# Byte offsets of split weights and activations in SBUF, and moved waits, in a one-core transformer kernel

## The reference

```
x = x + rms(retention(rms(x)))          # 4 heads; then x += (p0 @ W) * sigmoid(x @ Wg)
x = x + rms(latent_attention(rms(x)))   # 16 heads; then x += (p1 @ W) * sigmoid(x @ Wg)
mod = silu(c) @ w_ada + b_ada           # six rows of 1024 for shift, scale and gate
h = layer_norm(x) * (1 + sc1) + sh1
a, u, gates = h @ w_in                  # a: value and gate; u: 512 channels to be pooled
ya = silu(ln(conv31(a_val * sigmoid(a_gate)))) @ w_pw    # causal, depthwise, 31 taps, 512 channels
yb = multiscale_pool(u) @ w_pool * pool_scale
x = ln(ALPHA * x + g1 * ((sig(ga) * ya + sig(gb) * yb) @ w_out))
x = ln(ALPHA * x + g2 * ((gelu(gt) * v) @ w_down))       # v, gt from a conv with 3 taps of h @ w_up
```

## Time and profile before

| | |
|---|---|
| time, median of 3 runs | 846.46 us (845.76 to 847.8) |
| the profiled execution's own time | 850.78 us |
| its span, first to last instruction | 848.9 us |
| PE busy | 824.6 us (97%) |
| DVE, ACT, POOL busy | 664.1, 452.8, 46.8 us |
| data moved | 170.56 MB, mean 201 GB/s |

### The profile page before, as it was taken

How to read it: one execution, slowest core, us unless ns; L and a number is a source line. 1 busy time by engine, 2 the same in 40 slices (tenths; PEclk the granted TensorE clock), 3 DMA queues, 4 the chain that set the end, 5 groups by cost and what they waited for, 6 DMA issues and landing times.

```text
span 848.9 us, 14927 instructions
## 1 busy us (share of the span) xinstructions
PE 824.6 (97%) x5362; PEld 744.6 (88%) x5362; DVE 664.1 (78%) x1039; ACT 452.8 (53%) x678; POOL 46.8 (6%) x58
## 2 busy tenths in 40 slices
PE   9699999999999999999999999999999999999996
PEld 9598989888787999999987889988988999999884
DVE  5669896976874796877867777999798888888456
ACT  6353546464654656566565545202852877776440
POOL 0006300000010000000000000080000000000000
PEclk9899999999999999999999999999999999999998
DMA  6766684759754665564739662444663565566641
GB/s 236 258 219 223 199 286 168 271 182 351 262 172 152 217 224 183 192 231 143 271 112 359 203 238 86 162 156 148 212 208 126 185 211 189 182 203 217 196 151 50
DMA packets 49001, 170.56 MB, mean 201 GB/s; under 512 B 6080, under 2 KB 6720, under 8 KB 48960
## 3 DMA queue, kind: packets, MB, share of 16 engines
q1 hardware_dynamic: 40896, 143.23, 49.8%
q10 hardware_dynamic: 8064, 26.78, 9.0%
HBM read 168.93 MB, written 1.06 MB: 200 GB/s over the span
## 4 chain that ended last, share of the span: by engine, by line
PE 88%; DVE 4%; ACT 4%; DMA 2%; issue 1%; ACTq 0%; SPq 0%; DVEq 0%
PE bank L485 13%; PE bank L487 13%; PE bank L486 13%; PE bank L553 9%; PE bank L555 9%; PE bank L554 9%; PE bank L521 6%; PE bank L499 2%; PE bank L690 2%; PE bank L691 2%; PE bank L692 2%; DMA ada_raw<-ada_in 1%; PE bank L596 1%; PE bank L831 1%; DMA crow<-c_row 1%
## 5 line engine op out<-in xcount | busy, mean ns | idle before, releaser
L967 ACT ACTIVATE whi<-raw 128x1024 fp32r<-128x1024 f32 (+1 forms) x232 | 239.8, 1040 | 215.1 <-PE bank L487 92.4
L1492 DVE TENSOR_TENSOR wlo<-raw,whi 128x1024 fp32r<-128x1024 f32 (+1 forms) x232 | 278.3, 1212 | 74.3 <-ACT whi L967 72.8
L485 PE MATMUL bank<-H,whi 128*128 128x256 f32 x784 | 222.4, 284 | 0.1
L487 PE MATMUL bank<-H,wlo 128*128 128x256 f32 x784 | 219.4, 280 | 0.0
L486 PE MATMUL bank<-H,whi 128*128 128x256 f32 x784 | 218.6, 279 | 0.0
L485 PEld LDWEIGHTS bank<-H,whi 128*128 128x128 f32 x784 | 147.4, 188 | 1.0 <-issue 0.9
L486 PEld LDWEIGHTS bank<-H,whi 128*128 128x128 f32 x784 | 147.5, 188 | 0.1
L487 PEld LDWEIGHTS bank<-H,wlo 128*128 128x128 f32 x784 | 147.3, 188 | 0.0
L553 PE MATMUL bank<-whi,Y 128*128 128x512 f32 x216 | 86.0, 398 | 1.4 <-DVE wlo L1492 1.4
L555 PE MATMUL bank<-whi,Y 128*128 128x512 f32 x216 | 85.4, 395 | 0.0
L554 PE MATMUL bank<-wlo,Y 128*128 128x512 f32 x216 | 85.4, 395 | 0.0
(11 more groups left out here) (264 smaller groups left out, 1345.5 us busy)
## 6 DMA issues: line engine op xcount, KB each, us to landing
ada_raw<-ada_in ACTq DMA_DIRECT2D x48, 512.0 KB, 5.0
raw<-w_head SPq DMA_DIRECT2D x47, 512.0 KB, 4.4
raw<-w_up SPq DMA_DIRECT2D x42, 512.0 KB, 3.7
raw<-w_down SPq DMA_DIRECT2D x22, 512.0 KB, 4.3
raw<-w_uq SPq DMA_DIRECT2D x24, 384.0 KB, 3.1
raw<-w_ret_out SPq DMA_DIRECT2D x16, 512.0 KB, 5.5
raw<-w_mla_gate SPq DMA_DIRECT2D x16, 512.0 KB, 4.4
raw<-w_mla_out SPq DMA_DIRECT2D x16, 512.0 KB, 4.5
```

The lines of the kernel that those rows point to most:

```text
L485: mm(o, whi[:, s, c], a[:, 0, :], start=start, stop=False)
L487: last = mm(o, wlo[:, s, c], a[:, 0, :], start=False, stop=stop)
L967: activation(parts_of(b, n)[0], block_in(b, n), ACT.Copy).then_inc(hi_done, 1)
L1492: tt(lo, block_in(b, n), f32(hi), ALU.subtract).then_inc(lo_done, 1)
```

## The change

- `whi` and `wlo` get slots of 1088 elements instead of 1024 (4352 bytes). Blocks used as strips are written 16 elements (64 bytes) into their slot; `row_block` tells the row blocks, which are written at its first byte.
- `macc` grows from 32 to 256 bytes, so that the activations start at the same remainder by 256 as the slots.
- DVE's wait for `crow` moves from ahead of the first head into `ada`.
- In `out_rows` one `ada` goes behind `post_rows` and the next split, and the first two splits of `B_MO` move into the last head group, on ACT and on DVE; ACT takes two gate evacuations ahead of `turned(2)` there.
- At `B_MIN` the transposes of the second token tile start before the last half of the first pass's last block.
- PE's wait for `dve_free` before the groups moves into the group, ahead of the scores.
- Four blocks of `B_WG` (8 to 11) turn from plain products into strips: SP loads them, ACT and DVE split them, the last 14 taps interleaved with three of these splits. `conv_mean` comes behind the third of the eight strips, `conv_squares` behind the fifth.
- The running total of the taps is kept in PSUM (`CT`), and the last tap writes `CO`.

```diff
-        whi = sb("whi", [P, RING, 1024], F32R)
-        wlo = sb("wlo", [P, RING, 1024], F32R)
+        whi = sb("whi", [P, RING, 1024 + SLOT_PAD], F32R)      # SLOT_PAD, STRIP_AT = 64, 16
+        wlo = sb("wlo", [P, RING, 1024 + SLOT_PAD], F32R)
-        macc = sb("macc", [P, 8])
+        macc = sb("macc", [P, 64])
+        CT = PB[2][:].rearrange("p (c t) -> p c t", c=4)
+def row_block(b):
+    if b < B_RO:
+        return b % 12 in range(4, 8)
+    if B_GRP <= b < B_MO:
+        return (b - B_GRP) % 12 == 1
+    return b < B_MIN + 8 or B_MO <= b < B_WA or B_WO <= b < B_UP or b >= B_DN + 5
...
-            return whi[:, b % RING, 0:n], wlo[:, b % RING, 0:n]
+            o = 0 if row_block(b) else STRIP_AT
+            return whi[:, b % RING, o:o + n], wlo[:, b % RING, o:o + n]
...
-            load_plain_loop(B_WG, "gates", 4, 4)
+            load_plain_loop(B_WG, "gates", 3, 4)
+            load_some(B_WG, "gates", 12, 16)
...
-                    c = slice(t * P, t * P + P)
+                    c = slice(STRIP_AT + t * P, STRIP_AT + t * P + P)
...
-            token_pass(B_MIN, 0, 0, H, 0, 4, tile_waits(U_PRE1, 0))
-            turn_tile(U_PRE1, 1, WT, PB[1])
+            (blocks 0 to 2 of the pass, then:)
+            row_products(B_MIN + 3, half(2, 0, 0), 0, H, 6, False, True, (0,))
+            turn_tile(U_PRE1, 1, WT, PB[1], (0,))
+            row_products(B_MIN + 3, half(2, 0, 0), 0, H, 6, False, True, (1,)).then_inc(tok_done, 1)
+            turn_tile(U_PRE1, 1, WT, PB[1], (1,))
...
-            with pe.Fori(0, 3) as i:
+            with pe.Fori(0, 2) as i:
                 (four plain_tokens of B_WG)
-            conv_mean()
-            for j in range(12, 16):
+            for j in range(8, 16):
                 strip(B_WG + j, halves(b)[j % 2], H)
-                if j == 13:
+                if j == 10:
+                    conv_mean()
+                if j == 12:
                     conv_squares()
...
# ACT and DVE, out_rows:
-                    if base != B_RO or j > 1:
+                    if j > 1:
                         split(base + j)
# DVE:
+                dve.wait_ge(c_loaded, 16)        # in ada
...
-                    if j == 12:
-                        ada(ada0 + 6, 0, 6, 0, 0)
                 dve.wait_ge(row_a, loaded)
                 post_rows(n_root, 0, row)
                 split(base + 13)
+                ada(ada0 + 6, 0, 6, 0, 0)
...
-            dve.wait_ge(c_loaded, 16)            # ahead of the first head
...
+                        total = CO if per == 0 and k == CONV_K - 1 else CT
+                        stt(total[:, c, :], x, w_tap, CT[:, c, :], ALU.mult, ALU.add).then_inc(conv_tap[c], 1)
...
-            with dve.Fori(0, 7) as i:
+            with dve.Fori(0, 6) as i:
                 (14 taps)
+            for k in range(4):
+                if k < 3:
+                    split(B_WG + 5 + k)
+                (the last 14 taps, three or two a round behind each split)
...
             tt(CS[:, 0, :], CS[:, 0, :], CS[:, 1, :], ALU.add).then_inc(conv_sum, 1)
+            split(B_WG + 8)
```

More of the change, by code:

```diff
@@ L546, in loaded, with row_products @@
                 pe.wait_ge(lo_done, base + RING + 1)
-            def row_products(base, o, t, a, k0, start, stop):
+            def row_products(base, o, t, a, k0, start, stop, ks=(0, 1)):
                 hi, lo = parts_of(base)
-                for k in range(2):
+                for k in ks:
                     c = slice(512 * k, 512 * k + 512)
@@ L589, in hold, with turn_tile @@
                     mm(b[:, 0:P], ones[:], ones[:], start=True, stop=True)
[L591 to L593 removed]
+            def turn_tile(u, t, src, b, qs=(0, 1)):
+                for q in qs:
                     pe.wait_ge(wt_ready, 2 * (u + t) + q + 1)
@@ L736, in _ @@
                 row_products(B_PG0 + 4 + j, half(2, 1, 1), 1, H, 2 * j, j == 0, j == 3).then_inc(pe_done, 1)
-            token_pass(B_MIN, 0, 0, H, 0, 4, tile_waits(U_PRE1, 0))
-            turn_tile(U_PRE1, 1, WT, PB[1])
+            before = tile_waits(U_PRE1, 0)
+            for j in range(4):
+                loaded(B_MIN + j)
+                if j < len(before) and before[j]:
+                    pe.wait_ge(*before[j])
+                if j < 3:
+                    row_products(B_MIN + j, half(2, 0, 0), 0, H, 2 * j, j == 0, False)
+            row_products(B_MIN + 3, half(2, 0, 0), 0, H, 6, False, True, (0,))
+            turn_tile(U_PRE1, 1, WT, PB[1], (0,))
+            row_products(B_MIN + 3, half(2, 0, 0), 0, H, 6, False, True, (1,)).then_inc(tok_done, 1)
+            turn_tile(U_PRE1, 1, WT, PB[1], (1,))
             token_pass(B_MIN, 1, 0, H, 0, 4, tile_waits(U_PRE1, 1))
@@ L1323, in group @@
                     exps(3)
+                    split(B_MO)
+                    for j in range(2):
+                        gate_evac_one(base + 8 + j, j, 4 * o + 2 + j)
                     turned(2)
                     turned(3)
-                    for j in range(2):
-                        gate_evac_one(base + 8 + j, j, 4 * o + 2 + j)
+                    split(B_MO + 1)
                 act.wait_ge(mo_gated, at(5, 4))
@@ L1365, in _ @@
             evac(B_WP + 3, 1, U[:, 2:4, 16:16 + T], ACT.Copy)
-            with act.Fori(0, 2) as i:
-                evac(B_WG + 1, 0, dyn(G, 4 * i, 2), ACT.Sigmoid, 4, i)
-                evac(B_WG + 3, 1, dyn(G, 4 * i + 2, 2), ACT.Sigmoid, 4, i)
+            for n in range(3):
+                evac(B_WG + 2 * n + 1, n, pair(G, n), ACT.Sigmoid)
             act.wait_ge(pooled, 4)
             activation(Sh, PO, ACT.Copy).then_inc(pooled_hi, 1)
+            split(B_WG + 5)
+            split(B_WG + 6)
+            evac(B_WG + 7, 1, pair(G, 3), ACT.Sigmoid)
+            split(B_WG + 7)
+            split(B_WG + 8)
             evac(B_WG + 9, 0, pair(G, 4), ACT.Sigmoid)
```

22 lines of the change are left out of this document (14 added, 8 removed).

## The result

The changed kernel takes 824.75 us (median of 4, 823.85 to 828.66) against 846.61 us (median of 4, 845.76 to 847.8) in the same comparison: a ratio of 0.9749, 95% interval 0.9721 to 0.9778. It is 21.9 us faster. I had forecast 813.6 in a range from 796 to 832: the sign and the range hold, and the time is that of rival 3 (823) and not that of the forecast. The profiled execution has a span of 826.9 us, the longest of the five on record (the other four have 822.1 to 823.3). The profile of before, 850.78 us, is likewise of an execution above all its timed ones.

What follows compares the result with a forecast made beforehand. PE, busy 97% of the span, was taken as the bound. Addresses 17.8 - 0.5, `crow` wait 9.3, smaller pauses 2.7 and conv stage 3.6 sum to 32.9 us: from 846.46 to 813.6 us, range 796 to 832.

Steps and rivals of the forecast that it cites:

- rival 3: Only row blocks gain from the new addresses, strips stay at 116.7 ns a matmul; 823 us, chance 0.15.
- Rows of the address: Row blocks with moving operand in slots: 1176 matmuls of 512 columns gain 6.7 ns each, 7.8 us (0 to 20.3).
- Rival 1: The addresses do nothing, the kept blocks are fast for another reason; 831 us, chance 0.17.
- Strips of the address: Strips: 3000 matmuls of 256 columns go from 116.7 to 113.3 ns, 10.0 us less (0 to 26).
- split between strips and rows: Sign of a wrong forecast in the profile after: matmul pace unchanged, or differing between strips and row blocks.
- Rival 2: An address mismatch explains all PE lacks to the plain pace; 785 us, midway 799; chance 0.20 in whole or part.
- The wait for `crow`: PE's pause at 28.65 us and the half clock behind it: 7.4 + 2.4 - 0.5 = 9.3 us gained (6.9 to 9.8).
- Smaller pauses: PE's short waits before the projection, at `B_MIN` and at `B_MO`: together 2.7 us gained (1.5 to 3.2).
- Conv stage: Four plain blocks become strips, taps in PSUM avoid POOL's cost, the wait before `B_PW` goes: net 3.6 us gained.
- The overlap: Address gain lost where another engine sets the end: some 0.5 us in the conv stage, room elsewhere.

## Why the prediction was right, and where it was off

**Rows of the address: right.** 6.7 ns for 512 columns, in every block whose moving operand has the remainder of the activations. I counted 1176 matmuls and overlooked that five blocks of `B_DN` keep the strips' place: (1176 - 120) x 6.7 = 7.1 us instead of 7.8. Rival 1 falls.

**Strips of the address: the step that failed.** "I take the kept pace per column, 113.3 ns, since a remainder by 64 is then equal too: 3000 x 3.3 = 10.0 us." Two things are wrong in it. The reason: an equal remainder is no merit in strips; at 0 it is the worst (120.0). And both ends: the base was 116.7 from one strip of another stage, where the up stage ran at 117.7 already, and the new pace is 113.3 in 52 of 129 blocks and 117.8 in 77. The base alone would have made the gain larger; it is the new pace that made it small. By the means it was 3000 x (117.2 - 116.1) = 3.3 us in the profiled execution; 4.3 more if the up stage runs at the quicker pace. The prediction's own sign of being wrong, a pace "split between strips and rows", is what came. The bounds (0 to 26) held both. Rival 3 forecast the time by a mechanism that was half right: 64 bytes are no better than 32 in most blocks, and better in some. That its 823 is so near is luck: it had 15.6 us for the waits and the conv stage, which gave 11.5, and nothing for the strips. Rival 2 falls: nothing came near 108.

**The wait for `crow`: right in mechanism, a term too large.** 9.3 forecast, 6.8 measured alone. The step is "PE stands from 28.65 to 36.29": that was one late landing, the latest of fourteen profiles, in an execution 4.3 us over its kernel's median. By the middle landing, some 1.8 of the 2.5 us are that (an estimate). The forecast then took the whole of the 32.9 us off the median (846.46 - 32.9 = 813.6), as if that excess held none of the pause. PE now stands 0.7 us there against 0.5 forecast; the clock stays full; the `ada` with the wait holds nobody.

**Smaller pauses: right.** 0.57 + (0.97 - 0.29) + (1.43 - 0.28) = 2.4 us against 2.7.

**Conv stage: right in mechanism, a little less.** From the first plain record to `B_PW` it was 611.14 - 545.66 = 65.5 us and is 591.20 - 528.34 = 62.9: 2.6 us against 3.6. With the addresses of before it is 62.5, and with strips at 120.0 ns (at 0 bytes) 62.0: in this stage a quicker strip is worth nothing, since PE then waits for DVE, as below. Taps at 0.395 us beside POOL, as forecast (0.40). DVE is in time for the first new split. The pause that I put at the strip of block 11 (0.6 us) stands in two parts, at the means ahead of it (L620, 0.5) and at that strip (0.4). By the "GPSIMD Engine Reference" (Specifications) of the Trainium skill, contention is with instructions that have two SBUF inputs; the trace agrees in both directions, 29 taps with two inputs in SBUF and 44 with one in the same 17 us.

**The overlap: a cost at almost nothing.** The prediction lost 0.5 us of the addresses' gain to other engines, in the conv stage, and said of the rest: "Elsewhere there is room". The kernel without the addresses and the changed one have the same 5394 records of PE in one order, so their traces can be laid side by side, step by step (spans of 833.7 and 826.9 us). The steps that differ by less than 0.04 us, which are the paces of rows and strips, add up to 10.2 us less. The others give 3.4 us back: most are places where PE, being quicker, now comes before another engine is done. The largest are 0.64 us at `conv_mean`, 0.45 at 88 us, 0.33 and 0.28 at 26 and 30 us, and 0.26 and 0.25 ahead of transposes. With the second profile of the changed kernel the two figures are 11.0 and 4.5.

**The sum.** Waits and conv stage are 11.5 us for 15.6 forecast; the addresses are 10.2 by the medians for 17.3. In the pair of profiles the addresses are only 6.8, since that changed kernel had its whole up stage at 117.8; 4.3 more would make 11.1. Of the 11 us between 32.9 and 21.9, reckoned for the quicker up stage, some 2.4 are the strips (10.0 against 3.3 + 4.3), 2.9 the waits that came back, 2.5 the pause at `crow`, 0.7 the five blocks and 1 the conv stage and small pauses. The rest, some 1.5 us, stays open: these terms come from single profiles and the total from medians.

## What to carry to other kernels

Before a pace is multiplied by thousands of instructions, read it in each stage where these stand, and in the largest first: one strip at 400 us did not speak for the 40 blocks behind 650. A pause that waits for a transfer is as long as one execution made it; take it against the median before you count on it. A quicker pace of the busiest engine is partly given back as waits for the others, here 3.4 of 10.2 us. A cover that lets PE stand for some us also costs the clock behind it. Operand addresses are worth a try in matmuls at this precision, but stationary and moving operands want different places, and a place is chosen by measuring each, as here with one constant.

## What the runs showed of the hardware

- The same matmul of split operands has a pace that depends on where its operands begin: moving 512 columns, 226.7 ns with equal remainders by 256 bytes and 233.3 with 32 or 64 bytes between; moving 256 columns, 120.0 ns with equal remainders, 118.3 with the tile at 32 and the moving operand at 0, 116.5 to 117.9 with these two exchanged, 113.3 or 117.8 with the tile at 64 and at 192, 118.7 or 120.0 at 128.
- The paces 113.3 and 117.8 are held: in 348 stretches without a gap none changed, and a step longer by 0.17 us than its neighbours (656.21 to 656.49) could part 113.3 from 117.8 for the 36 blocks that followed.
- The Trainium skill ("TensorE: Matmul & The Clock Gate", back-to-back issue gap) gives 109 and 216 ns for these shapes and names no address among the conditions. No run here brought the split products to it; the plain records stay there (34.69 us / 160 = 217 ns, with the tail of the last).
- DVE accumulating into PSUM costs no more than into SBUF without POOL (0.395 us for a tap of 256 columns), and POOL's work beside it costs nothing: 44 taps in 17 us with it, 43 without.
- After PE had stood 5.42 us the granted clock was 0.50 from 568 to 572 us, and 24 steps of 256 columns took 5.25 us instead of 2.72.
